# Thirteen instead of nine Strassen pairs in a decoder step's input projection, and a new order from up to down projection

## The reference

```
h  = rmsnorm(x, g_mix_pre)
z  = h @ w_in                            # 7168 columns: rq rk rv rg | dq dk dv
ret = retention(rq, rk, rv, rg)          # 8 heads of 128, chunks of 128, carried state
dif = diff_attention(dq, dk, dv)         # 4 heads, two softmaxes each; the sample
                                         # tokens attend to 2 pages of 128 cached keys
x += rmsnorm(concat(ret, dif) @ w_out)
x += rmsnorm(cross_attention(rmsnorm(x), 256 memory tokens) )
x += rmsnorm(square(relu(rmsnorm(x) @ w_up)) @ w_down)   # 2048 -> 8192 -> 2048
```

## Time and profile before

| | |
|---|---|
| median of 3 runs | 2866.84 us (2866.24 to 2868.13) |
| the profiled execution, its own time | 2870.36 us |
| its span, first to last instruction | 2868.7 us |
| busy: PE, PEld | 2789.5 us (97%), 2562.7 us (89%) |
| busy: DVE, ACT, POOL | 2087.2 us (73%), 1097.8 us (38%), 276.5 us (10%) |
| mean granted clock of PE | 0.988 |
| the chain that ended last | PE 82%, DVE 8%, issue 5%, DMA 2% |

### The profile page before, as it was taken

The page is one execution under the profiler, slowest core; times in us unless marked ns, Lnnn a source line. Parts: engine busy times, 40 slices in busy tenths (PEclk is TensorE's granted clock), DMA queues, the critical chain, the costliest instruction groups (busy, mean ns, idle before and its releaser), DMA issues.

```text
span 2868.7 us, 48373 instructions
## 1 busy us (share of the span) xinstructions
PE 2789.5 (97%) x18690; PEld 2562.7 (89%) x18690; DVE 2087.2 (73%) x2655; ACT 1097.8 (38%) x1376; POOL 276.5 (10%) x444
## 2 busy tenths in 40 slices
PE   7999999999999999999999999999989999999998
PEld 7899998999899999778899999999978888888887
DVE  6799854555466654746887777777778888888886
ACT  6333333223233323443544444444443333333332
POOL 0000013112222100000000000000010000000000
PEclk9999999999999999999999999999999999999999
DMA  6443465455567645252254444444453534444353
GB/s 219 152 115 115 124 190 176 142 167 167 182 207 232 208 163 166 65 156 74 104 162 145 144 139 149 141 148 145 134 192 126 163 100 141 153 134 150 99 178 132
DMA packets 387828, 430.36 MB, mean 150 GB/s; under 512 B 13750, under 2 KB 300716, under 8 KB 385516
## 3 DMA queue, kind: packets, MB, share of 16 engines
q1 hardware_dynamic: 345960, 269.19, 31.4%
q0 software_dynamic: 41504, 159.26, 16.0%
q10 hardware_dynamic: 228, 0.06, 0.0%
HBM read 342.21 MB, written 86.25 MB: 149 GB/s over the span
## 4 chain that ended last, share of the span: by engine, by line
PE 82%; DVE 8%; issue 5%; DMA 2%; ACT 1%; POOL 1%; POOLq 0%; DVEq 0%; SPq 0%; ACTq 0%
PE gemm L2909 23%; PE aux L3019 4%; PE gemm L3019 4%; PE aux L3021 4%; PE aux L3020 4%; PE gemm L3021 4%; PE gemm L3020 4%; PE gemm L3600 3%; PE gemm L3601 3%; PE gemm L3602 3%; PE aux L3600 3%; PE aux L3602 3%; PE aux L3601 3%; PE aux L3065 1%; PE gemm L2995 1%
## 5 line engine op out<-in xcount | busy, mean ns | idle before, releaser
L2909 PE MATMUL gemm<-act_hi,w_hi 128*128 128x288 f32 x1968 | 441.2, 306 | 4.2 <-DVE act_lo L2383 2.8
L2909 PE MATMUL gemm<-act_hi,w_lo 128*128 128x288 f32 x1968 | 422.2, 296 | 0.0
L2909 PE MATMUL gemm<-act_lo,w_hi 128*128 128x288 f32 x1968 | 421.9, 296 | 0.0
L2909 PEld LDWEIGHTS gemm<-act_hi,w_hi 128*128 128x128 f32 x1968 | 315.3, 189 | 34.7 <-issue 23.7
L2909 PEld LDWEIGHTS gemm<-act_hi,w_lo 128*128 128x128 f32 x1968 | 317.8, 189 | 0.0
L2909 PEld LDWEIGHTS gemm<-act_lo,w_hi 128*128 128x128 f32 x1968 | 317.7, 189 | 0.0
L1691 ACT ACTIVATE w_hi<-w_raw 128x2048 fp32r<-128x2048 f32 x60 | 115.1, 1919 | 308.4 <-PE aux L3602 178.1
L2555 DVE TENSOR_TENSOR w_lo<-w_raw,w_hi 128x1024 fp32r<-128x1024 f32 x120 | 146.6, 1222 | 108.5 <-ACT w_hi L1614 108.5
L1801 DVE TENSOR_TENSOR w_lo<-w_raw,w_hi 128x2048 fp32r<-128x2048 f32 x71 | 162.4, 2288 | 57.0 <-ACT w_hi L1182 56.4
L1182 ACT ACTIVATE w_hi<-w_raw 128x2048 fp32r<-128x2048 f32 x71 | 136.0, 1916 | 123.5 <-PE gemm L2909 64.7
L2649 DVE TENSOR_TENSOR w_lo<-w_raw,w_hi 128x2048 fp32r<-128x2048 f32 x60 | 137.3, 2289 | 24.0 <-ACT w_hi L1691 23.0
(11 more groups left out here) (525 smaller groups left out, 7407.3 us busy)
## 6 DMA issues: line engine op xcount, KB each, us to landing
w_raw<-in_w_mlp_up SPq DMA_DIRECT2D x120, 512.0 KB, 4.2
w_raw<-in_w_in SPq DMA_DIRECT2D x37, 1024.0 KB, 5.8
w_raw<-in_w_mlp_down SPq DMA_DIRECT2D x32, 1024.0 KB, 6.3
side_hi<-in_w_mlp_down SPq DMA_DIRECT2D x32, 1024.0 KB, 7.2
w_raw<-in_w_in SPq DMA_DIRECT2D x38, 512.0 KB, 4.2
w_raw<-in_w_out SPq DMA_DIRECT2D x16, 1024.0 KB, 6.5
u_sum_scratch<-u_sum POOLq DMA_DIRECT2D x32, 512.0 KB, 2.9
z_scratch<-z_out SPq DMA_DIRECT2D x56, 288.0 KB, 2.3
```

The lines of the kernel that those rows point to most:

```text
L2909: ins = M(out[half][:, 0:TH], w[b][:, cols], x[:, k, half * TH:(half + 1) * TH], start=first and n == 0, stop=last and n == 2)
```

## The change

Thirteen pairs instead of nine, by four pairs more of retention v and gate tiles of heads 0 to 3; the list alternates turned pairs (6, 8, 10, 12, 14) with unturned ones. Filler falls from six to four tiles per differential head (HT), counted in eighths of a tile (12 matmuls): the remaining 24 filler tiles are q and k of retention heads 0 to 3 and all of heads 4 to 7. So all four filler tiles of the first two differential heads are turned, and the first two of the other heads. In a head, DVE's tile_end(1) stands in block 1, none in block 2 (where d_low moves to, from block 3), tile_end(2) after block 3, tile_end(3) after atn and tile_end(4) at the end. The page numbers are read by POOL at the start instead of ahead of the first d_load. At the transition from up to down ACT copies v_e1 and splits the first stripe before the operands, DVE takes the first stripe first and T1 before S1, and POOL loads A12, As2, S2, S4 and S3 later; SP swaps the third and fourth stripe.

The constants:

```diff
-HT = 6
+HT = 4
-IN_PAIRS = 9
-IN_TURNED = 5
+IN_LIST = [16, 6, 18, 8, 20, 10, 22, 12, (0, 2), 14, (2, 2), (0, 3), (2, 3)]
+IN_PAIRS = len(IN_LIST)
+IN_TILES = [[(ZR + p + f, p + f) if isinstance(p, int) else (p[1] * RH + p[0] + f, ZD + 4 * (p[0] + f) + p[1]) for f in range(2)]
+            for p in IN_LIST]
+IN_ROT = [isinstance(p, int) and p < 16 for p in IN_LIST]
+FILL = [4 * h + g for h in range(RF) for g in range(2)] + list(range(4 * RF, ZR))
...
-d_fill = [(2, 3), (4, 5, 6), (7, 8, 9), (10, 11, 12)]
+d_fill = [4, 7, 10, 13, 16]
```

SP, the first down stripes:

```diff
             sp.wait_ge(v_m, 7 * ALL_PAIRS - 1)
+            d_load(d21, 0, 1, 0, in21)
             d_load(d22, 0, 1, 1, in22)
-            d_load(d21, 0, 1, 0, in21)
```

POOL, at the start and before the first d_load:

```diff
+            pool.wait_ge(s_pg, 16)
+            page = [pool.value_load(pg[0:1, i:i + 1], min_val=0, max_val=NPOOL - 1) for i in range(DB * NPG)]
...
-            pool.wait_ge(s_pg, 16)
-            page = [pool.value_load(pg[0:1, i:i + 1], min_val=0, max_val=NPOOL - 1) for i in range(DB * NPG)]
```

POOL, the transition:

```diff
-            for name in ("A11", "S1", "As1", "A12", "S2"):
+            for name in ("A11", "As1", "S1"):
                 u_load(0, name)
+            s_store(pair(UP_PAIRS - 2))
+            pool.wait_ge(v_m, 7 * ALL_PAIRS)
             pool.wait_ge(u_h, u_count(0, "As1"))
+            u_load(0, "A12")
             u_load(0, "As2")
-            s_store(pair(UP_PAIRS - 2))
-            pool.wait_ge(v_m, 7 * ALL_PAIRS - 1)
+            v_store(pair(UP_PAIRS - 1))
+            pool.wait_ge(s_wlo, w_count(0, 0, 1))
+            u_load(0, "S2")
             u_load(0, "S4")
             u_load(0, "S3")
-            v_store(pair(UP_PAIRS - 1))
             s_store(pair(UP_PAIRS - 1))
```

ACT, the transition:

```diff
+            v_copy(pair(UP_PAIRS), v_e1, A[0], 7 * ALL_PAIRS - 2, 6 * ALL_PAIRS - 5)
+            w_high(0, 0, 0, 0)
             u_high(0, "A11")
             u_high(0, "S1")
             u_high(0, "As1")
-            v_copy(pair(UP_PAIRS), v_e1, A[0], 7 * ALL_PAIRS - 2, 6 * ALL_PAIRS - 5)
-            w_high(0, 0, 0, 0)
+            v_copy(pair(UP_PAIRS), v_u3, A[0], 7 * ALL_PAIRS, 6 * ALL_PAIRS - 2)
+            w_high(0, 0, 0, 1)
             u_high(0, "A12")
-            w_high(0, 0, 0, 1)
-            v_copy(pair(UP_PAIRS), v_u3, A[0], 7 * ALL_PAIRS, 6 * ALL_PAIRS - 2)
-            v_square(pair(UP_PAIRS), 0, 6 * ALL_PAIRS + 2)
             w_high(0, 0, 0, 2)
+            v_square(pair(UP_PAIRS), 0, 6 * ALL_PAIRS + 4)
```

DVE, a differential head (tile_end(2) now follows block 3, tile_end(3) the copy of atn, tile_end(4) the end of the head):

```diff
-                    elif qb < PC - 1:
-                        tile_end(qb)
-                    elif h:
+                    elif qb == 1:
+                        tile_end(1)
+                    elif qb == 2 and h:
                         d_low(h - 1)
-                tile_end(3)
+                tile_end(2)
...
-                tile_end(4)
...
-                tile_end(5)
+                tile_end(3)
...
-                tile_end(6)
+                tile_end(4)
```

DVE, the transition:

```diff
+            w_low(0, 0, 0, 0)
             u_low(0, "A11")
+            t_add(0, 0, "T1")
             u_low(0, "S1")
             u_low(0, "As1")
             v_join(tail, v_cf[0][:, TH:T], A[2], v_e1, ((v_m, tail(7, -1)), (v_e, tail(4, 1)), (v_s, tail(2, -1))))
-            w_low(0, 0, 0, 0)
-            t_add(0, 0, "T1")
-            u_low(0, "A12")
-            w_low(0, 0, 0, 1)
-            v_relu(tail, 0, tail(6, 1))
...
+            w_low(0, 0, 0, 1)
+            u_low(0, "A12")
+            v_relu(tail, 0, tail(6, 1))
             v_relu(tail, 1, tail(6, 4))
             w_low(0, 0, 0, 2)
             u_low(0, "S2")
```

PE, the filler in eighths:

```diff
-                fill(0)
+                fill(0, 2)
...
-                fill(1)
+                fill(2, 4)
...
-                        fill(*d_fill[qb])
+                        fill(d_fill[qb], d_fill[qb + 1])
```

More of the change, by code:

```diff
@@ L58 @@
 ZE = 6
-IN_PAIRS = 9
-IN_TURNED = 5
+IN_LIST = [16, 6, 18, 8, 20, 10, 22, 12, (0, 2), 14, (2, 2), (0, 3), (2, 3)]
[3 more added lines that the diff above has]
+IN_ROT = [isinstance(p, int) and p < 16 for p in IN_LIST]
+IN_TURNED = sum(IN_ROT)
+IN_HEAD = IN_LIST.index(8)
+FILL = [4 * h + g for h in range(RF) for g in range(2)] + list(range(4 * RF, ZR))
+FILL_TURNS = [sum(r % 4 < 2 for r in FILL[:i]) for i in range(len(FILL))]
+ZB = ZE // 2 + IN_PAIRS
 ZQ = ZT - 2 * IN_PAIRS
@@ L652, in program @@
         IN0 = 16 * ALL_PAIRS
+        V_S0 = 2 * (IN_PAIRS - IN_TURNED) + 2
         UIN0 = DH * 2 * 16 * NPG
@@ L751, in _, with fill_load @@
                 in_load(p, 0, 0)
-            def fill_load(r):
+            def fill_load(i):
+                r = FILL[i]
                 col = r % 4 * RH + r // 4
@@ L765, in _ @@
                 in_store(IN_PAIRS - 1, f)
-            for r in range(2, ZR):
+            for r in range(2, len(FILL)):
                 sp.wait_ge(s_wlo, S_IN + ZE + r - 1)
@@ L967, in r_load_z @@
                 for b in range(2):
-                    pool.wait_ge(s_zst[b], 16 * (ZD // 2 + 2 * h + 2))
+                    pool.wait_ge(s_zst[b], 16 * (ZB + (h + 1 if h < RF else 2 * h - 2)))
                 pool.dma_start(r_zin[h % 2][:], zr[h]).then_inc(r_zin_full[h % 2], 16)
@@ L1347, in _ @@
                         d_high(h - 1)
-                    if s in (3, 5, 7):
-                        split((s - 1) // 2)
+                    if s in (3, 7):
+                        split((s + 1) // 4)
                 for p in range(DB // 2):
@@ L1367, in _ @@
                                                accum_out=d_sum[:, 8:9]), "sexp")
-                split(5)
+                split(3)
                 act.wait_ge(D_PE.sem, D_PE.of("ss", h))
@@ L1981, in i_turn @@
             def i_turn(k, f, made):
-                if k >= IN_TURNED:
+                if not IN_ROT[k]:
                     return
-                n = 2 * k + f
+                n = 2 * sum(IN_ROT[:k]) + f
                 z = z_out[f][0:32, :].rearrange("p (a t) -> p a t", a=2)
@@ L2210, in r_head @@
                 first = ZE + 4 * HT + 2 * h
-                stored = 16 * ((ZD + 4 * HT + 2 * h) // 2)
-                turns = (first - ZE) // 4 * 2
-                part = (first - ZE) % 4
+                stored = 16 * (ZB + 2 * HT + h)
                 def own(name, ins):
@@ L2277, in r_head @@
                 if h < RF - 1:
-                    z_ret(first, 0, stored, part, turns + part)
+                    z_ret(first, 0, stored, FILL[first - ZE] % 4, FILL_TURNS[first - ZE])
                 elif h >= RF:
@@ L2307, in r_head @@
                     own("lo", V.tensor_tensor(r_ylo[:], r_y[:], r_yhi[:].bitcast(F32), ALU.subtract))
-                    z_ret(first + 1, 1, stored, part + 1, turns + part + 1)
+                    z_ret(first + 1, 1, stored, FILL[first + 1 - ZE] % 4, FILL_TURNS[first + 1 - ZE])
                 else:
@@ L3068, in _, with fill, fill_half @@
             with pe.Fori(0, DH) as h:
-                def fill(*quarters):
-                    for q in quarters:
-                        for part in range(2):
-                            fill_half(q, part)
-                def fill_half(q, part):
-                    j, part = q // 4, 2 * (q % 4) + part
+                def fill(first, end):
+                    for n in range(first, end):
+                        fill_half(n)
+                def fill_half(n):
+                    j, part = n // 8, n % 8
                     if part == 0:
```

48 lines of the change are left out of this document (23 added, 25 removed).

## The result

The changed kernel takes 2884.25 us (median of the runs) against 2866.84 us: ratio 1.0061, 95% interval 1.005 to 1.0073. It is slower by 17.4 us. The forecast was 2863.3, its range 2853 to 2879. The profiled execution took 2885.7 us. One of the five executions took 3167.8 us at a mean granted clock of 0.81 and stands apart; without it the median is 2883.6.

A forecast was written before the change was run, and what follows sets the result against it. TensorE was taken as the bound, busy 97% of the span. Tiles and pairs -18.2, page numbers -4.6, heads +16.8, pages +4.0, transition -1.5 sum to -3.5 us: 2863.3 us from the median 2866.8, range 2853 to 2879.

The forecast's parts named there:

- Pairs: Input stage: four more pairs cost 89.1 us, less 5.1 us as turned pairs stop losing time; net 84.0 us.
- The d_z wait: First head: reading page numbers earlier removes a 2.85 us wait and 1.7 us of clock loss, together -4.6 us.
- The norm5 wait: Third block of each differential head: TensorE waits 2.6 us for DVE, whose work no longer fits under thinner filler.
- Its clock: Behind the norm5 wait in each head: 1.6 us lost to a lower clock, bounds 0 and 1.7.
- key pages 4 and 5: In each head: still just in time, costed at nothing; some 2 us per head if a 1 MB load collides.
- The value pages: Pages 6 and 7 in each head: thinner cover costs 1.0 us per head, 4.0 in all, bounds 0 and 1.6.
- page loads as the bound of a head: Rival, differential heads: both page waits grow by 2.5 us per head, 20 us in all, 2883 us; chance 0.21.
- the transition: Up to down projection: idle time moved more than removed, -1.5 us; bounds -14.2, or +3 if S2 lands late.
- As2 ready 0.5 to 1.5 us earlier: Transition, third down product: its operand As2 would be ready that much before the 2127.34 of the kernel before.
- the rival in which the new order pays: Transition: the new order removes both waits, 14.2 us instead of 1.5, giving 2850.6 us; chance 0.13.
- thinner filler would eat it: Differential heads: less filler exposes DVE work, costing 4.2 us per head, 16.8 in all; 2863 us, chance 0.42.
- a bound of 86 us for a head: Sign of error: heads of about 82 to 83 us expected; under 80 or over 86 would refute the forecast.

The follow-up runs named there:

- dve_order: Changed kernel with DVE's head work spread anew (split in block 2, d_low last) and one eighth of filler moved to the third block: 2876.53 us, ratio 1.0036.
- loads_wait: Changed kernel with SP holding two 1 MB weight loads per head until key, respectively value, pages 4 to 7 have landed: 2861.84 us, ratio 0.9988.
- early_z: Changed kernel with POOL fetching d_z for the next head after the scores sn, not after the last value pages: 2885.78 us, ratio 1.0075.
- split_first: Changed kernel with DVE splitting the third filler tile before taking the second out of PSUM, after the fourth block: 2894.02 us, ratio 1.0106.
- after_again: The changed kernel run once more, unaltered, as reference of its group: 2883.39 us, ratio 1.0064.
- best_c: Changed kernel with dve_order, loads_wait, POOL's wait for stored output moved behind key pages 4 to 7, and S2 loaded right behind As2: 2844.02 us, ratio 0.9921.
- pages_early: The kernel before with one edit, POOL reading the sixteen page numbers at its start: 2859.98 us, ratio 0.998.

## Why the prediction was wrong

**Right.** Pairs: +84.0 forecast, +83.5 measured, no exception among them. The d_z wait: gone; the same edit alone brings 5.9 us (forecast 4.6; part of it is that the two waits for value pages in the kernel before, 2.3 us, became one of 0.8). The norm5 wait: 2.6 us forecast, 2.7 to 3.1 measured, in all four heads, from a walk of DVE's chain with the durations of before. That it is DVE's order and not DVE's total that makes it, dve_order shows. Its clock: 1.6 us forecast; where it stands alone, in loads_wait, the granted clock falls four times in the heads, once behind each norm5 wait, and windows of 2 us add up to 6.8 us lost, 1.7 each.

**Wrong: key pages 4 and 5 costed "at nothing".** The forecast found their cover just in time, wrote that a collision with a weight load of 1 MB would cost some 2 us per head, and then left it out of the sum. It happens in every head: by the new place of tile_end(2), the load goes out with the pages (503.96 and 504.94). The value pages got the same treatment: 1.0 us per head for thinner cover, nothing for the weight load. The row the term rests on, the wait of 0.82 us in the earlier trace rows, was itself such a collision, and was read as thin cover alone. In the kernel before, SP's load goes out 0.2 us ahead of the pages of 672.66:

```profile
672.44 0.37 SPq L636 DMA_DIRECT2D w_raw<-in_w_in  x1
...
d_vp<-in_cache_diff_v POOLq DMA_DIRECT2D x4, 128.0 KB, 5.8
```

Page waits of 6.3 us in all were forecast (2.3 as before and 4.0), 14.5 measured: 8.2 us. That the load is the cause, and not d_z behind the pages, early_z (d_z moved, nothing won), split_first (load closer, 10.6 us worse than after_again) and loads_wait (load held, 21.6 us better) show together. The nearest rival, page loads as the bound of a head at 2883 us with 0.21, had the place and the cause; I ranked it too low. That it also has the time is in part luck: it counted 20 us of page waits above the sum, where 8.2 came, and the clock and the transition brought the rest.

The Trainium skill (DMA: Bandwidth & Descriptors, "Queues, rings and completion order") says that each DMA engine takes turns between its queues; a page on POOL's queue then has to share with a weight load on SP's. With that the trace agrees: 2.3 to 2.7 us alone, 4.2 to 7.0 beside 1 MB.

**Wrong: the clock counted behind norm5 alone.** In the heads of the changed kernel the granted clock fell eight times: behind all four norm5 waits, and behind four of the ten waits on pages. Seven falls cost 1.7 us each, the first one 3.4; while TensorE was busy they cost 14.4 us in all, where the forecast had 6.4. Without them its busy time would be 317.2 - 14.4 = 302.8 us, close to the 406.1 - 1.7 - 102.2 = 302.2 of the forecast's terms. The error of 17.6 us is then 8.2 of page waits, 0.8 of norm5 (11.2 against 10.4), 8.0 of clock and 0.6 of rest. Best_c can't serve as the measure of these heads without clock loss: its clock never falls and the same 2380 matmuls are busy for 305.0 us. The four kernels with the order of dve_order have 304.9 to 305.7 us of busy time besides what the clock took, the seven with the changed kernel's order and matmuls 302.3 to 303.4; why is not shown. The Trainium skill (TensorE: Matmul & The Clock Gate, "HAM oscillation — how this bites in real kernels") tells of a wait that recurs and is paid for with a throttled restart each time. Here 8 of the 14 waits were paid for so, in after_again 6, in split_first 5.

**Wrong: the transition,** -1.5 forecast, +2.1 measured to the third down product. The idle time was moved and not removed, as forecast, and the last product starts on time. The step that failed is "As2 ready 0.5 to 1.5 us earlier": S2, ahead of it in DVE's order, is loaded only behind the stores of the last pair, the case named in the bound "S2 lands late, +3". Eleven profiles of the changed kernel and its variants agree, the new order (eight of them) with 1342.8 to 1344.4 us for that stretch, the old one (three) with 1340.1 to 1340.5, so that 3 us is nearer than 2.1; the two kernels with nine pairs have 1341.3 (before) and 1339.0 (pages_early). With S2 loaded in time the new order is the better one by 3 us (1337.1). So the rival in which the new order pays had something in it, behind one misplaced load.

**Where the gain went.** The forecast held that thinner filler would eat it. But best_c has the same thirteen pairs and four filler tiles, and its heads take 309.1 us, where the forecast had 411.75 - 86.0 = 325.8: less by the norm5 term of 16.8. One sign of being wrong was set too wide: a bound of 86 us for a head allows 344 us for the four, 18 above the sum, and the 343.4 measured pass it. The gain was not bound to be eaten by the thinner filler. It was given back in the order of DVE's work, in SP's weight loads and in POOL's loads at the transition, and edits of a few lines to each repair that.

## What to carry to other kernels

When work is taken out from under a DMA, ask first what else is issued in the same microsecond, and only then how much cover is left: the cover can be ample for a transfer alone and too little for one beside 1 MB. A load with slack of its own is best held until the urgent one has landed. A collision that the working names as possible belongs in the sum with a place in time (which instruction frees each of the two), not in a clause.

## What the runs showed of the hardware

- In the changed kernel half a page of 128 KB lands in 2.3 to 2.7 us alone, and in 4.2 to 7.0 us when it is issued within 3 us behind a load of 1 MB on another queue. Right behind a store of 288 KB, with no load of 1 MB near, it takes 3.7 to 5.2 us (loads_wait).
- The length of an idle stretch of about 2 us does not decide whether the granted clock drops: the same wait of 1.88 to 1.90 us left it at 0.67 in one execution and at 1.00 in another. Where it fell to 0.50, some 1.7 us were lost as a rule, and over 3 us behind the first norm5 wait of the changed kernel. The same heads with the same waits took 343.4, 338.9 and 337.2 us.
- Work of no use, 18 matmuls per head in place of idling, saved about 7 us in the whole kernel; the granted clock fell three times in the heads instead of six to eight.
